# An mLSTM block's last four z tiles as two Strassen pairs, with the residual reread in three parts

## The reference

```python
cq, ckv, k_rope, mq, mk, mv, mo, gates, z = split_cols(u @ w_in, EVEN_SPLITS)
...
def combine(a, h, mo, z, dtype):
    hm = head_rmsnorm(jax.nn.sigmoid(mo.astype(jnp.float32)) * merge_heads(h), h_norm, MLSTM_HEADS).astype(dtype)
    return (jnp.concatenate([merge_heads(a), hm], axis=-1) * jax.nn.silu(z)) @ w_out
...
h_lat = h_lat + gate_l[:, None] * y_lat
h_ctx = h_ctx + gate_c * y_ctx
```

## Time and the profile before

| what | value |
|---|---|
| time, median of 3 | 4127.57 us (4126.22 to 4130.86) |
| the profiled execution: its time | 4125.18 us |
| its span | 4123.4 us |
| mean granted TensorE clock | 0.99 |
| PE busy | 4012.5 us (97%) |
| the tail's last five products (chunks 53 to 57), z4 to z7, up to the projection | from 1026.89 to 1132.16 us |
| the projection | from 1132.16 us, 137.66 us long |

### The profile page before, as it was taken

The page is one execution under the profiler, slowest core; times in us unless marked ns, Lnnn a source line. Parts: engine busy times, 40 slices in busy tenths (PEclk is TensorE's granted clock), DMA queues, the critical chain, the costliest instruction groups (busy, mean ns, idle before and its releaser), DMA issues. The chain is left out here.

```text
span 4123.4 us, 47350 instructions
## 1 busy us (share of the span) xinstructions
PE 4012.5 (97%) x18122; PEld 2410.0 (58%) x18122; DVE 1730.2 (42%) x4000; ACT 951.5 (23%) x1770; POOL 558.4 (14%) x535
## 2 busy tenths in 40 slices
PE   7999999999899999989999999999999999999998
PEld 4686666777457658667644466656544444444447
DVE  3236665577114256746437512222533252222234
ACT  4223332232103411135314411111121010000001
POOL 0000000100000110132004112122100021221122
PEclk9999999999999999999999999999999999999999
DMA  5320001211202121232112111122243111111113
GB/s 208 134 77 7 8 8 20 65 59 39 91 24 80 34 67 47 62 121 78 42 71 76 62 44 60 46 69 84 97 174 115 51 31 46 46 41 41 51 41 103
DMA packets 113568, 270.19 MB, mean 66 GB/s; under 512 B 15479, under 2 KB 45033, under 8 KB 112254
## 3 DMA queue, kind: packets, MB, share of 16 engines
q1 hardware_dynamic: 106368, 251.81, 18.5%
q0 software_dynamic: 5920, 13.25, 1.3%
q10 hardware_dynamic: 1056, 2.10, 0.1%
HBM read 218.53 MB, written 50.87 MB: 65 GB/s over the span
## 5 line engine op out<-in xcount | busy, mean ns | idle before, releaser
L426 PE MATMUL upper_banks<-sbuf 128*128 128x512 f32 (+1 forms) x2016 | 771.4, 545 | 1.5 <-issue 1.1
L2972 PE MATMUL upper_banks<-sbuf 128*128 128x512 f32 x1400 | 615.2, 595 | 4.5 <-ACT sbuf L3231 3.1
L426 PEld LDWEIGHTS upper_banks<-sbuf 128*128 128x128 f32 x2016 | 382.4, 190 | 388.8 <-issue 374.0
L2972 PEld LDWEIGHTS upper_banks<-sbuf 128*128 128x128 f32 x1400 | 262.8, 191 | 315.9 <-issue 307.6
L2237 PE MATMUL gla_prod<-sbuf 128*128 128x512 f32 x560 | 247.5, 593 | 0.3 <-DVE sbuf L2269 0.3
L582 DVE TENSOR_TENSOR sbuf<-upper_banks,sbuf 128x512 f32<-128x512 f32 (+1 forms) x140 | 81.8, 584 | 283.2 <-PE upper_banks L426 282.7
L977 PE MATMUL mla_banks<-sbuf 128*128 128x512 f32 (+1 forms) x416 | 176.0, 511 | 0.0
L2237 PEld LDWEIGHTS gla_prod<-sbuf 128*128 128x128 f32 x560 | 104.5, 192 | 119.9 <-issue 117.4
L378 POOL TENSOR_TENSOR sbuf<-sbuf 128x512 f32<-128x512 f32 x36 | 47.1, 1308 | 904.5 <-POOLq L68 331.7
L3472 DVE TENSOR_TENSOR sbuf<-upper_banks,sbuf 128x512 f32<-128x512 f32 x75 | 53.6, 715 | 222.7 <-PE upper_banks L2972 214.3
L1160 ACT ACTIVATE sbuf<-mla_banks,sbuf 128x1280 f32<-128x1280 f32 (+1 forms) x80 | 92.6, 1158 | 216.2 <-DVE sbuf L1278 142.8
(11 more groups left out here) (515 smaller groups left out, 6315.3 us busy)
## 6 DMA issues: line engine op xcount, KB each, us to landing
sbuf<-in_l_w_in SPq DMA_DIRECT2D x59, 512.0 KB, 3.9
sbuf<-in_w_in SPq DMA_DIRECT2D x52, 512.0 KB, 4.5
sbuf<-in_w_mlp_out SPq DMA_DIRECT2D x40, 512.0 KB, 3.6
sbuf<-in_w_mlp_in SPq DMA_DIRECT2D x32, 512.0 KB, 3.6
sbuf<-in_l_w_mod SPq DMA_DIRECT2D x24, 512.0 KB, 5.2
scratch_gates<-sbuf SPq DMA_DIRECT2D x48, 256.0 KB, 2.0
sbuf<-scratch_gates SPq DMA_DIRECT2D x8, 1536.0 KB, 7.3
sbuf<-in_l_w_mod SPq DMA_DIRECT2D x8, 1024.0 KB, 15.1
```

The lines of the kernel that those rows point to most:

```text
L426: last = nc.tensor.matmul(bank_of(n, c)[:, 0:wd], lw[:, k * P:(k + 1) * P], right_operand(c, base, tw, k, o, wd, to), start=k == 0 and c i ...
L2972: last = nc.tensor.matmul(pb, lw[:, k * P:(k + 1) * P], rhs, start=k == 0 and c in ("P1", "P2", "P5"), stop=k == 3, skip_group_check=True)
```

## The change

The tiles z4 to z7 become two more pairs, (z4, z5) and (z6, z7), with the same `TURNS`. With them:

- The results of these pairs (`results`: ctx and the four of `GIVES`, five a pair) each get 4 transposes, a Silu and a multiplication. Those of P2, P7 and P3 are first added by VectorE into `zs`, and ScalarE then applies Silu in place there; ctx and P4 go from the bank through Silu to `zs` as before. VectorE's loop does the sum of a result ahead of the multiplication of the result before it (`gate_z(i - 1)`).
- GpSimd makes four weight sums for each new pair.
- `Tw(0..3)`, `kept` and `S1` are needed up to the last product, so H can't be read at z4 any more. Rows 0 to 2, which lie over `Tw(0)` and `Tw(1)`, are read once P5 of the last pair is done; rows 3 to 7 after the last chunk and the last sum. `h_in` becomes three semaphores, and VectorE waits for the first at row 0 of the projection, for the second at row 1, and for the third at row 3.
- Both attention outputs b = 2 and 3 are issued at z4's first chunk.
- ScalarE copies out P6 of (z2, z3), `evict(TAIL)`, ahead of `square(3)`, and P5 between the Silu of `y[0]` and that of `y[1]`; before, both came after the two Silus.

```diff
-        if (what == "mk" and j) or (what == "z" and j in (1, 3)):
+        if (what == "mk" and j) or (what == "z" and j % 2):
             continue
-        if (what == "mq" and j) or (what == "z" and j in (0, 2)):
+        if (what == "mq" and j) or what == "z":
...
-                if n == first_of[t] and what == "z" and j in (2, 4, 5):
-                    for b in {2: (0, 1), 4: (2,), 5: (3,)}[j]:
+                if n == first_of[t] and what == "z" and j in (2, 4):
+                    for b in {2: (0, 1), 4: (2, 3)}[j]:
...
-                    if j == 4:
-                        sp.wait_ge(chunked, last_pair)
-                        sp.wait_ge(dve_out, n_dve[NCH])
-                        for jj in range(KD):
-                            sp.dma_start(H[:, jj, :], io["h"][:, jj * T:(jj + 1) * T]).then_inc(h_in, 16)
+                if n == step_of[pairs[-1], "P7"]:
+                    sp.wait_ge(chunked, step_of[pairs[-1], "P5"] + 1)
+                    for jj in range(3):
+                        sp.dma_start(H[:, jj, :], io["h"][:, jj * T:(jj + 1) * T]).then_inc(h_in[min(jj, 1)], 16)
+            sp.wait_ge(chunked, NCH)
+            sp.wait_ge(dve_out, n_dve[NCH])
+            for jj in range(3, KD):
+                sp.dma_start(H[:, jj, :], io["h"][:, jj * T:(jj + 1) * T]).then_inc(h_in[2], 16)
...
+            evict(TAIL)
             square(3)
             act.drain()
-            act.wait_ge(dve_out, n_dve[first_of[pairs[-1]]])
-            for k in range(2):
-                nc.scalar.activation(y[k], y[k], ACT.Silu).then_inc(ysil, 1)
+            act.wait_ge(dve_out, n_dve[first_of[z2]])
+            nc.scalar.activation(y[0], y[0], ACT.Silu).then_inc(ysil, 1)
+            evict(TAIL + 1)
+            nc.scalar.activation(y[1], y[1], ACT.Silu).then_inc(ysil, 1)
...
-                act.wait_ge(chunked, n + 1)
-                if m >= 2:
-                    act.wait_ge(ymul, m - 1)
-                nc.scalar.activation(zs[:, m % 2, 0:wd], banks[:, n % 2, 0:wd], ACT.Silu).then_inc(act_out, 1)
+                if by_dve[n]:
+                    act.wait_ge(dve_out, n_dve[n + 1])
+                    nc.scalar.activation(zs[:, m % 2, :], zs[:, m % 2, :], ACT.Silu).then_inc(zsil, 1)
+                else:
+                    act.wait_ge(chunked, n + 1)
+                    if m >= 2:
+                        act.wait_ge(ymul, m - 1)
+                    nc.scalar.activation(zs[:, m % 2, :], banks[:, n % 2, :], ACT.Silu).then_inc(act_out, 1)
...
+            for i, n in enumerate(results):
+                if by_dve[n]:
+                    dve.wait_ge(chunked, n + 1)
+                    dve.wait_ge(act_out, n_act[n + 1])
+                    dve.drain()
+                    nc.vector.tensor_tensor(zs[:, i % 2, :], banks[:, n % 2, :], kept[ADDS[CH[n][5]]], ALU.add).then_inc(dve_out, 1)
+                if i:
+                    gate_z(i - 1)
+            gate_z(len(results) - 1)
...
-                if n == 0:
-                    dve.wait_ge(h_in, 16 * KD)
+                if p == 0 and j in (0, 1, 3):
+                    dve.wait_ge(h_in[(0, 1, None, 2)[j]], (16, 32, None, 80)[j])
```

More of the change, by code:

```diff
@@ L1375, in mlstm_block @@
     n_act = [n - n_dve[n] for n in range(NCH + 1)]
-    last_pair = step_of[pairs[-1], "P4"] + 1
-    z4 = TILES.index(("z", 4))
+    z2 = TILES.index(("z", 2))
+    plain_end = step_of[z2, "P4"] + 1
+    results = [n for n in range(plain_end, NCH) if CH[n][5] == "ctx" or CH[n][5] in GIVES]
     orders = [list(range(TT)), [1, 0] + list(range(TT - 1, 1, -1))]
@@ L1424, in mlstm_block @@
         sgd, hmd, sqd, ssd, rooted, normed = (s.sem(c) for c in ("sgd", "hmd", "sqd", "ssd", "rooted", "normed"))
[L1425 removed]
+        osqd, added, ssum, rootc = (s.sem(c) for c in ("osqd", "added", "ssum", "rootc"))
+        h_in = [s.sem(f"h_in{i}") for i in range(3)]
         a_in = [s.sem(f"a_in{i}") for i in range(2)]
@@ L1448, in place, with heads @@
             return y[j + late][:, NCTX + lo:NCTX + lo + 512], src
+        def heads(n):
+            k, c = CH[n][2] - 4, CH[n][5]
+            if c == "ctx":
+                return [(k + i, b) for i in range(2) for b in range(2)]
+            return [(k + GIVES[c][0], (NCTX + GIVES[c][1]) // P + a) for a in range(4)]
         @block.sync
@@ L1624, in _ @@
                 chunk(n)
-                t, what, k, o, wd, c = CH[n]
-                if k < 4:
+                if n not in results:
                     continue
-                pe.wait_ge(normed, k - 3)
                 if m >= 2:
                     pe.wait_ge(ymul, m - 1)
-                for a in range(wd // P):
-                    last = nc.tensor.transpose(banks[:, 2 + m % 2, a * P:(a + 1) * P], hs[:, k - 4, o // P + a, :], ident[:])
+                for a, (k, b) in enumerate(heads(n)):
+                    pe.wait_ge(normed, k + 1)
+                    last = nc.tensor.transpose(banks[:, 2 + m % 2, a * P:(a + 1) * P], hs[:, k, b, :], ident[:])
                 last.then_inc(y_tr, 1)
@@ L1978, in _ @@
             plain(1)
-            for n in range(TAIL, last_pair):
+            for n in range(TAIL, plain_end):
                 add(n)
@@ L1983, in _, with gate_z @@
             plain(3)
[L1984 to L1992, removed]
+            def gate_z(i):
+                n = results[i]
+                k, c = CH[n][2], CH[n][5]
+                dve.wait_ge(y_tr, i + 1)
+                if by_dve[n]:
+                    dve.wait_ge(zsil, sum(by_dve[a] for a in results[:i + 1]))
+                else:
+                    dve.wait_ge(act_out, n_act[n + 1])
+                if c == "ctx":
+                    parts = [(k, 0, slice(0, NCTX)), (k + 1, 0, slice(NCTX, 2 * NCTX))]
+                else:
+                    parts = [(k + GIVES[c][0], NCTX + GIVES[c][1], slice(0, 512))]
+                for j, o, r in parts:
+                    last = nc.vector.scalar_tensor_tensor(out=y[j][:, o:o + r.stop - r.start], in0=banks[:, 2 + i % 2, r], scalar=g[:, j - 4:j - 3],
+                                                          in1=zs[:, i % 2, r], op0=ALU.mult, op1=ALU.mult)
+                last.then_inc(ymul, 1)
+                if c in ("P3", "P4"):
                     dve.drain()
                     dve.sem_inc(ydone, 1)
+            for i, n in enumerate(results):
+                if by_dve[n]:
+                    dve.wait_ge(chunked, n + 1)
+                    dve.wait_ge(act_out, n_act[n + 1])
+                    dve.drain()
[3 more added lines that the diff above has]
+            gate_z(len(results) - 1)
             def add_square(n):
```

10 lines of the change are left out of this document (5 added, 5 removed).

## The result

| | before | after |
|---|---|---|
| time, median | 4127.71 us (4 executions, 4126.22 to 4130.86) | 4099.48 us (4 executions, 4098.73 to 4105.91) |
| the profiled execution: its time, its span | 4125.18, 4123.4 us | 4098.73, 4096.9 us |
| start of P6 in the tail | 1026.89 | 1031.02 |
| from there to the projection | 105.27 | 83.84 |
| from there to the end of the span | 2991.2 | 2982.0 |

The last three lines show where to look. The stage gained 21.43 us, as forecast; TensorE's work ahead of the stage and from the projection on is the same in both kernels, and yet 4.1 us were lost ahead of the stage and 9.2 gained behind it.

A forecast was written before the change was run, and what follows sets the result against it. TensorE, busy 97% of the span, was taken as the bound; -6.87 - 3.46 - 1.65 - 7.89 - 1.47 + 0.15 = -21.2 us took the median from 4127.57 to 4106, range 4101.5 to 4112.

The forecast's parts named there:

- Fewer matmuls: In the tail's new pairs, eight matmuls of 512 columns fall away on TensorE's path: -6.87 us.
- The first wait and its slow spell: TensorE's idleness before P7 of (z2, z3) goes, -3.46 us, and the lower clock behind it, -1.65.
- +0.15 at P4: New TensorE wait at P4 of (z2, z3), because VectorE adds P7 only at about 1041.0: +0.15 us.
- The second wait and its slow spell: TensorE's idleness before the transposes of z4's last chunk goes, -7.89 us, and the lower clock behind it, -1.47.
- New results: Sum, Silu and multiplication of the new pairs' results stay hidden behind TensorE's products: nothing, at most about 1 us a product.
- GpSimd's sums: Eight weight sums of 1.27 us each for the new pairs are ready before TensorE needs them: nothing.
- H at nothing: H's rows, read later around the projection's start, land before VectorE's lateness could hold up TensorE: no cost.
- Rivals 1 to 5: P4 waits 4111.5 (0.06); slow spells stay 4109.5 (0.03); read-out waits 4120 (0.06); H late 4111 (0.03); products' clock falls 4154 (0.02).
- ScalarE's table load: Before the tail's Silus: 1.28 us without drain, by the row; with the page's drain the sum would be -19.8.
- the spread of the runs: Whole kernel's execution times, 4.6 us between lowest and highest, used with unknown handovers to give 4102 to 4110.
- should only shift: The 3000 us after the changed stage were taken to move in time only, with no time lost there.
- the two slow spells: TensorE at the lower clock right after each of the tail's two waits, 1.65 and 1.47 us, forecast to go.

The follow-up runs named there:

- The second comparison: The unedited changed kernel run once more against the kernel before: median 4106.32 us (5 executions), ratio 0.9950.
- the shifted kernels: The kernel before with 2 or 4 extra matmuls of unused result ahead of the projection: 4125.44 and 4129.65 us, ratios 1.0002 and 1.0009.

## Why the prediction was right in the stage and wrong in the sum

**Fewer matmuls, -6.87.** Right: 90.7 against 83.8 us of stage with and without them, and 6.87 when eight are put back.

**The first wait and its slow spell, -5.1, and +0.15 at P4.** Right in the stage: 5.2 come back with the old order of copies. P4's new wait is 0.2 at most. Alone, the edit gave 4.2, because the spell behind the next wait grew by 1.6 while that wait shrank by 0.7.

**The second wait and its slow spell, -9.4.** Right: 9.3 alone. (Read from start to start, the spell in the earlier trace rows is 1.43 and not 1.47: the transposes took 0.88 instead of 0.44, a loss of 0.44.) Both together 14.6 against 14.3.

**New results, GpSimd's sums and H at nothing.** Right, with the margins worked out: no engine made TensorE wait, the clock stayed at 1.00, and H landed before anyone asked. Rivals 1 to 5 did not happen. ScalarE's table load, for which the Trainium skill's page ScalarE: Activation LUTs (What ACT_TABLE_LOAD costs) states a drain of 1380 ns besides, again was followed by the Silu at once (1037.44 + 1.28, Silu at 1038.74). So that term was rightly taken from the row.

**What failed is the step from the stage to the time**: "the spread of the runs (4.6 us between lowest and highest)", taken from three executions, and with it the assumption that the 3000 us behind the stage "should only shift"; in the first pair of traces they gained 9.2 us. All 76 times of the kernel before, over all comparisons, run from 4118.89 to 4134.55, mean 4126.87, with a standard deviation of 4.4; the 15 of the changed kernel from 4095.78 to 4111.15, mean 4102.85 and median 4102.09, deviation 4.5. The difference of the means is 24.0, with a 95% interval of 1.96 x sqrt(4.4^2/76 + 4.5^2/15) = 2.5 either way, so 21.5 to 26.5. Against it the forecast of 21.2 is low by 2.8, and the first comparison's 28.2 high by 4.2: that the first median fell outside the range is in good part chance. The second comparison gave 22.1 (4128.40 - 4106.32). A range of 4101.5 to 4112 was drawn from 4.6 us where the medians of four to six executions of this same kernel were 4099.5, 4106.3 and 4101.2.

The traces show part of what scatters, and that it is in code that the change does not touch. The first product of the mLSTM stage follows a wait of 1.49 us in both first traces; before the change:

```profile
707.68 34.61 PE L1573 MATMUL mls_banks<-sbuf 128*128 128x256 f32 x96 [1.49 <-PEq L68]
```

and in the changed kernel:

```profile
709.07 37.35 PE L1584 MATMUL mls_banks<-sbuf 128*128 128x256 f32 x96 [1.49 <-PEq L68]
```

The same 48 matmuls (96 records, chunks of 256 and 512 columns in one row), the same wait for TensorE's own sequencer (PEq), 2.7 us apart; granted clock 1.00 from 700 to 720 in the one, 0.81 in the other. Neither value belongs to a kernel. From this product to P6 eight of the fourteen traces have 319.2 us, three of them with the pairs, and six have 321.9 to 322.1, two of them without. Over the traces of all fourteen executions profiled, the first product of the attention stage starts between 39.5 and 44.9 us and P6 between 1023.5 and 1035.6, in code that is the same in all.

A part of the excess can be said to follow from the change, and it is a term of the sum that was sized too small: the two slow spells, 1.65 + 1.47 = 3.1 us, were read from one trace. In the four traces in which both waits stand they took 3.1, 3.2, 5.6 and 5.7, on average 4.4, while the second wait was 7.89 in the first and 7.1 to 7.4 in the others. So the stage of the kernel before was 105.3, 104.9, 107.2 and 107.2 us in four traces (the last two with the added matmuls not counted), on average 106.2, while the stage without waits was 83.8 or 83.9 in six. That makes 22.3 us for the stage. What remains to 24.0 is within the interval. Whether a systematic microsecond or three is left stays open: from the start of the projection on, seven traces of kernels without the pairs average 2989.0 us and seven with the pairs 2986.1, with a spread in the latter of 2982.0 to 2991.4. That a clean stretch is not bound to the pairs was shown for the stretches above by the shifted kernels. Why the clock fell in one execution and not in another was not shown.

One thing was argued and not tried. In the changed kernel b = 3 could not have stayed behind z4, since VectorE's sums for z4's pair stand behind `plain(3)`, and SP would wait for those sums. The early output is not an extra there but needed.

No run beat the changed kernel; the 4102.00 of the one with two idle matmuls more, five executions, is within its scatter.

## What to carry to other kernels

Price a wait of TensorE with the clock behind it, but as a range: here 3.46 us cost between 1.6 and 3.2 more, and 7.1 to 7.9 between 1.4 and 3.0 more, from trace to trace. Before giving a range for the time, ask how it scatters; three executions within 4.6 us hid a scatter of 16, and a gain of some microseconds is proved sooner by the length of the changed stage in two traces (83.84 twice) than by medians, as long as the stage has no waits and the rest of the kernel does not change. And read a DMA that is waited for first by when it was issued: here moving 5.45 us of transfer ahead in the queue was worth more than the faster algorithm.

## What the runs showed of the hardware

**Slow-clock spells differ for one and the same wait.** Behind 1.49 us of idleness 96 records took 34.61 us in one trace and 37.35 in another; behind 7.89 us 16 records took 4.60, behind 7.22 they took 6.16. The Trainium skill's page TensorE: Matmul & The Clock Gate (What's actually happening) states that the clock's observation runs freely and not from the kernel's start, so that the same kernel meets it at different places. These rows agree with it, without proving it.

**A slow spell with no idle time before it.** A stretch in which the profile shows TensorE busy throughout can have one: 75 us all busy at 0.95 in the kernel before, at 1.00 in the changed one. In the kernel before the clock was 1.00 up to 2066.80. It was lower in the next 10 us, which follow the start of a row of matmuls with a single output column (the row, then the two stretches):

```profile
2065.41 4.32 PE L3983 MATMUL upper_banks<-sbuf 128*128 128x1 f32 x32
2066.80:2071.80 5.00, 5.00 (x24) 0.64 0.20 46
2071.80:2076.80 5.00, 5.00 (x9) 0.68 0.93 377
```

In the changed kernel the same row took 3.63 us and the clock stayed at 1.00, so such a row is not followed by a spell each time.

**GpSimd held up by VectorE, or the other way round.** One of GpSimd's sums took almost twice its usual time:

```profile
1055.74 2.44 POOL L1532 TENSOR_TENSOR sbuf<-sbuf 128x512 f32<-128x512 f32 x1 [16.05 <-PE mls_banks L1557]
1059.62 1.27 POOL L1535 TENSOR_TENSOR sbuf<-sbuf 128x512 f32<-128x512 f32 x1 [1.44 <-PE mls_banks L1573]
```

It began at 1055.74, when VectorE was multiplying two operands from SBUF (1054.01 to 1057.06), and ended 1.12 after that. The Trainium skill's page SBUF — State Buffer (Who interferes with whom) says that a VectorE `tensor_tensor` with both inputs in SBUF contends with GpSimd's reads. The row agrees; it cost nothing, since P7 needed that sum only at 1070.1. In the changed kernel's second trace it is VectorE whose rows are longer, 3.97 us for the two multiplications that took 3.05 in the first, while the same sum took 1.48:

```profile
1054.95 3.97 DVE L1990 TENSOR_TENSOR sbuf<-sbuf 128x1280 f32<-128x1280 f32 x2 [7.08 <-DMA sbuf<-scratch_ao]
1056.09 1.48 POOL L1532 TENSOR_TENSOR sbuf<-sbuf 128x512 f32<-128x512 f32 x1 [16.05 <-PE mls_banks L1557]
```
